# Scan groups of a hybrid decoder layer: rows spread over the partitions by transfers from memory in place of matmuls, with a new order inside a group

## The chip, the cores and the metric

The kernel runs on one core of a Trainium2 chip. The metric is the device time of one execution in microseconds (us), as the median of several runs. The engines are TensorE (PE; its weight loads are PEld), VectorE (DVE), ScalarE (ACT), GpSimd (POOL) and SyncE (SP), which issues nearly all DMAs from one queue, in program order. A wait in that queue holds back everything behind it. All data are float32, and each matmul of the program stands in the trace as two instructions.

## The reference, cut to what matters

One step of a decoder layer: 512 prompt tokens and 8 decode tokens (T = 520 columns) go through a sparse attention branch and a Mamba-2 scan branch, are merged, and pass a feed-forward block. The change is in the scan branch, which has 8 groups of 4 heads of 64 channels, with a state size of 128:

```python
xbc = silu(causal_conv(xbc_pad, conv_w, conv_b))          # x, B and C of the group, 4 taps
a_cum = cumsum(dt_c * A, axis=2)                          # in chunks of 128 tokens
L = exp(where(tri, a_cum[:, :, :, None] - a_cum[:, :, None, :], -inf))
CB = einsum('bclgn,bcsgn->bclsg', C_c, B_c)
y_diag = einsum('bclsg,bclsgr,bcsgrp->bclgrp', CB, L, xdt)
# chunk after chunk, h is the state:
y_off = einsum('blgn,bgrpn,blgr->blgrp', Ck, h, exp(ak))
h_new = h * exp(ak[:, -1]) + einsum('blgn,blgr,blgrp->bgrpn', Bk, exp(ak[:, -1:] - ak), xk)
# the 8 decode tokens, each with a state of its own:
h = h * exp(dtt * A) + einsum('bgrp,bgn,bgr->bgrpn', xt, Bt, dtt)
y = einsum('bgrpn,bgn->bgrp', h, Ct)
# both, per group:
y = (y + d_skip * xs) * silu(z)
y = y * rsqrt(mean(y * y over the group's 256 channels) + EPS) * ssm_norm_w
```

## The kernel before, in words

Everything lies transposed, channels on the 128 partitions and tokens in the columns. The order is written out by hand for each engine and held together by semaphores. The stages are: norm and first projections, index scores and top-k, attention, the 8 scan groups, the products with `w_ssm_br` (`sbr`) and the gates, decode attention, and then the output and feed-forward products.

**A group.** While the scan of group g is computed, PE also computes the six dense tiles of the input projection of group g+1 (x, x, B, C, z, z), 16 matmuls each, as filler between the steps of the scan: `D(i)` is tile i, `D(i, k0, k1)` a part of its eight k steps. Two pairs of PSUM banks alternate, so a tile starts only when ACT has copied out the tile before the last (`tile_in`; `gate_ahead` in the last group). In the last group the filler is tiles of the gate projection (`last_tile`). PE's steps are:

- `step_aux`: small transposes (raw columns, old convolution rows, the state `hT` of the group before), and, with the selector matrix `gs`, matmuls that put dt and decay of the decode tokens (L972, L973) and the decays at the chunk ends (L977) on all partitions.
- `step_norm` (L417) sums the squares of the group before. ACT takes the root, DVE the reciprocal, and `spread_norm` (L425, L426) puts the result on all partitions for DVE's `norm`.
- `step_turn` transposes B and x of the chunks (L994, L999).
- `step_decode` (L1011) puts each decode token's B row and C row on all partitions, in PSUM banks 6, 7 and 4, 5, where DVE reads them (L1849, L1860).
- `step_cb` (L1019) is CB of the four chunks, masked by DVE into `CBm`.
- `step_a` (L1028), once per chunk, puts four heads' cumulated decay rows on all partitions in bank 4. ACT's `chunk` makes from them `M2` (L1418, L1422) and `Cx2` (L1420); POOL multiplies these with `CBm` and C (L2243, L2246).
- `step_y` (L1041, L1044, L1047), once per chunk, makes the output and the state increment. DVE carries the state on (`hT`, L1878 and L1881), and the next `step_y` waits for that (`h_done`).

DVE does, in this order: copies of the group's constants, 12 convolution taps (L1811), the exponent of the chunk weights (L1815), four silu products (L1818), part of a round of the decode top-k (L1770, L1776, L1779; nobody in the group waits for its result), `norm` of the group before, `xdt` and `xw`, the rest of the round, the decode state update (L1849, L1854) and output (L1860, L1863), `CBm`, a second round, four carries of the state with `z_gate` ahead of the last, and the group's output `Y`. ACT's `squares`, POOL's `add_squares` and PE's `step_norm` follow on `Y`. POOL also does the decode tokens' convolution (L2222 to L2232) and the decay of the decode states (L2237).

SP stores the convolution rows and states, loads the next group's state, rows and selectors, and loads the weights of group g+2 when their slots are free.

Of the kernel before, what the change touches and what calls it, by code (L numbers as in the profile page):

```python
# [26 lines left out]
P = 128  # L27
D = 1024
# [48 lines left out]
def build(nc, x_prompt, x_sample, cache_k, cache_v, cache_idx_k, state_ssm, state_conv, page_table,  # L77
# [5 lines left out]
    with ExitStack() as ctx:  # L83
# [19 lines left out]
        gs = sb("gs", [32, GSEL])  # L103
        vec = sb("vec", [P, 96])
        cwg = sb("cwg", [P, NG, 24])
# [98 lines left out]
        scratch = nc.dram_tensor("decode_scores", (NB, PAST), F32, kind="Internal").ap()  # L204
        iqslot = [ikt3, ikt1]
# [34 lines left out]
        scl = scl[0:24, :]  # L240
        smallg, sa = W(sa, 512)
# [17 lines left out]
        cw = G(24)  # L259
        dtg, atg = G(4, 4), G(4, 4)  # L260
        sct = G(4, 24)
        sc0, sc1, sc2, sc3 = G(4, NB), G(4, NB), G(4, NB), G(4, NB)
        dts, dAs, xdts, ys = G(2, NB), G(2, NB), G(2, NB), G(2, NB)
        alast, ealast = G(4, 4), G(4, 4)
        wexp = G(4, 4)
# [96 lines left out]
        GIDX_READY, IK_READY, IDX_ZERO, WK_READY, MASK_READY, RAW_ZERO = 7, 8, 9, 10, 11, 12  # L362
        QK_NEW_READY, ROWS_READY, LK_READY, DMAX_READY, DP_READY, DO_READY = 13, 14, 15, 16, 17, 18

        VEC_READY, TAPS_READY, DSK_READY, IK_SQ, IK_ROOT, QKVS_READY, IKTOK_READY = 1, 2, 3, 4, 5, 7, 9
# [46 lines left out]
        def sum_squares(pe, e, *squares):  # L412

            for b in range(5):
                n = P if b < 4 else NB
                for i, sq in enumerate(squares):
                    mm = pe.matmul(ps[0:n, 6, b:b + 1], sq[:, b * P:b * P + n], ones[:, 0:1],  # L417
                                   start=(i == 0), stop=(i == len(squares) - 1))
            mm.then_inc(S("norm_summed"), 1)
# [9 lines left out]
        def root_norm(act, e, n):  # L429

            act.wait_ge(S("norm_summed"), e + 1)
            for rows, cols in ((P, slice(0, 4)), (NB, slice(4, 5))):
                act.activation(rt[0:rows, cols], ps[0:rows, 6, cols], ACT.Sqrt, scale=1.0 / n,
                               bias=eps[0:rows, 0:1]).then_inc(S("norm_root"), 1)
# [6 lines left out]
        def copy_norm(act, e, out):  # L441
            act.wait_ge(S("norm_spread"), e + 1)
# [92 lines left out]
        def _(sp):  # L535
            sp.sem_inc(S("sout_out"), OPEN)
            sp.dma_start(cst[:, 0:2 * P], consts[:, 0:2 * P]).then_inc(S("ident_in"), 16)
# [35 lines left out]

            sp.wait_ge(S("dsc_ready"), OPEN + 16)
# [56 lines left out]
            def load_selectors(g):  # L631
                sp.dma_start(gs[:], gsel_d[bass.ds(g, 1)].rearrange("o p c -> (o p) c")
                             if not isinstance(g, int) else gsel_d[g]).then_inc(S("gs_in"), 16)
# [3 lines left out]
            load_selectors(0)  # L637
# [6 lines left out]
            def group_io(g, more, last=False):  # L644

                store_conv(g)
# [12 lines left out]
                if not last:  # L659
                    sp.wait_ge(S("abc_done"), 4 * g + 4)  # L660
                    load_selectors(g + 1)

            group_io(0, True)
            with sp.Fori(1, NG - 2) as g:
                store_prompt_state(g - 1)
                group_io(g, True)
            store_prompt_state(NG - 3)
# [4 lines left out]
            store_prompt_state(NG - 2)  # L672
# [8 lines left out]
            load_sbr(0, (N_SBR + 2, N_SBR + 4))  # L681
            store_prompt_state(NG - 1)
# [32 lines left out]
            load_ga(3, N_SBR + 14)  # L715
            load_att(0, N_SBR + 16)
# [37 lines left out]
        def _(pe):  # L754
# [204 lines left out]
            def step_aux(g, prev):  # L959
# [3 lines left out]
                if prev:  # L963
                    pe.wait_ge(S("h_done"), 4 * g)
                for i in range(4):
                    mm = pe.transpose(ps[0:11, 5, i * P:(i + 1) * P], raw[:, i, SEQ:SEQ + 11], ident)
                mm.then_inc(S("ctok_done"), 1)
                pe.wait_ge(S("scl_in"), 48 * g + 48)
                pe.wait_ge(S("gs_in"), 16 * g + 16)
                for j in range(2):  # L970
                    sel = gs[:, 512 + j * P:512 + (j + 1) * P]
                    pe.matmul(ps[:, 4, 96 + NB * j:96 + NB * (j + 1)], sel, dtT[0:32, SEQ:T], start=True, stop=True)  # L972
                    pe.matmul(ps[:, 4, 112 + NB * j:112 + NB * (j + 1)], sel, acT[0:32, SEQ:T], start=True, stop=True)  # L973
                for i in range(4):
                    mm = pe.transpose(ps[:, 4, i * 24:(i + 1) * 24], scl[:, i * P:(i + 1) * P], ident[0:24, 0:24])
                for r in range(4):
                    mm = pe.matmul(ps[:, 4, 384 + 4 * r:388 + 4 * r], gs[:, r * P:(r + 1) * P], acT[0:32, P - 1:SEQ:P],  # L977
                                   start=True, stop=True)
# [5 lines left out]
            def step_norm(g):  # L984

                pe.wait_ge(S("sqg_added"), g + 1)
                sum_squares(pe, g + 1, sqg[:, 0, :])

            def step_turn(g, prev):
# [5 lines left out]
                if prev:  # L995
                    pe.wait_ge(S("norm_copied"), 2 * g + 2)
# [6 lines left out]
            def step_decode(g):  # L1003

                pe.wait_ge(S("xdt_ready"), 2 * g + 2)
                pe.wait_ge(S("Bt_ready"), g + 1)
                pe.wait_ge(S("aux_read"), g + 1)
                pe.wait_ge(S("silu_done"), 4 * g + 4)
                for t, bank in ((2, 6), (3, 4)):
                    for b in range(NB):  # L1010
                        mm = pe.matmul(ps[:, bank + b // 4, (b % 4) * P:(b % 4 + 1) * P],  # L1011
                                       xc[:, t, SEQ + b:SEQ + b + 1].broadcast_to((P, P)), ident,
                                       start=True, stop=True)
# [1313 lines left out]
```

## Time and profile before

| | |
|---|---|
| median of 3 runs | 1694.37 us (1694.1 to 1696.58) |
| the profiled execution, its own time | 1695.87 us |
| its span, first to last instruction | 1694.1 us |
| PE busy | 1602.1 us, 95% of the span |
| DVE busy | 1007.6 us, 59% |
| ACT, POOL busy | 369.8 us, 218.4 us |
| mean granted TensorE clock | 0.965 of full speed |
| DMA | 131.14 MB, 77 GB/s over the span |

The span and the median are nearly the same, so a microsecond in the trace is a microsecond of the metric. A timeline row gives start, duration, engine, line, operation and operands, and in brackets the idle time ahead of it with the engine that ended it. Rows of PE overlap the next by about 0.07 us, since the ends of matmuls are modelled, so the start-to-start distance is the better cost.

### The profile page before, as it was taken

To read this page: it belongs to the slowest core of one execution; us is meant where nothing else is said; L and a number is where in the kernel's file an instruction comes from. 1 tells how busy PE (TensorE), PEld (TensorE's weight loads), DVE (VectorE), ACT (ScalarE), POOL (GpSimd) and SP (SyncE) were. 2 spreads that over 40 slices of the span, in tenths; PEclk is the share of its full clock that TensorE was granted. 3 is DMA by queue.
4 is the path that set the end of the run, shared out by engine and by line. 5 is a ranking of instruction groups with operands and counts; after the bars stand their busy time and mean duration, and the time that the engine had idled before them with its cause. 6 is when DMAs were issued, how large, how long until landed. Compare 5 with 4: busy or idle time off the path is not lost. (4 is left out here: it accounts for less than half of the span.)

```text
span 1694.1 us, 21865 instructions
## 1 busy us (share of the span) xinstructions
PE 1602.1 (95%) x8083; PEld 1356.9 (80%) x8083; DVE 1007.6 (59%) x1640; ACT 369.8 (22%) x817; POOL 218.4 (13%) x224
## 2 busy tenths in 40 slices
PE   6998998899999999999989999999999999999997
PEld 5886786788877787777877788888888888888885
DVE  3313886336868667686775897403786666667222
ACT  3112316422343433424232100010011000000002
POOL 1000110021322413224132000520000000000000
PEclk7999999999999999999999999978999999999997
DMA  6111114033133121331122322421322323220301
GB/s 207 50 38 51 37 51 115 12 91 100 57 104 101 57 74 57 101 88 48 50 82 75 123 79 75 138 86 55 96 75 75 99 74 99 75 92 21 129 9 51
DMA packets 153486, 131.14 MB, mean 77 GB/s; under 512 B 11411, under 2 KB 149939, under 8 KB 153411
## 3 DMA queue, kind: packets, MB, share of 16 engines
q1 hardware_dynamic: 150610, 121.93, 23.7%
q0 software_dynamic: 2816, 8.39, 1.7%
q8 instruction: 41, 0.67, 0.2%
q14 instruction: 19, 0.15, 0.0%
HBM read 117.26 MB, written 13.27 MB: 77 GB/s over the span
## 5 line engine op out<-in xcount | busy, mean ns | idle before, releaser
L389 PE MATMUL ps<-xn,ring 128*128 128x260 f32 (+1 forms) x2752 | 638.1, 389 | 6.0 <-ACT work L1316 1.9
L389 PEld LDWEIGHTS ps<-xn,ring 128*128 128x128 f32 (+1 forms) x2752 | 522.9, 193 | 91.9 <-ACT work L1316 2.3
L469 PE MATMUL ps<-uT,ssm_o 128*128 128x260 f32 x616 | 139.5, 383 | 0.1
L469 PEld LDWEIGHTS ps<-uT,ssm_o 128*128 128x128 f32 x616 | 117.0, 190 | 18.4 <-issue 0.4
L389 PE MATMUL ps<-ssm_o,ring 128*128 128x260 f32 x512 | 114.0, 386 | 0.0
L389 PEld LDWEIGHTS ps<-ssm_o,ring 128*128 128x128 f32 x512 | 98.3, 192 | 15.3
L469 PE MATMUL ps<-xn,ring 128*128 128x260 f32 x392 | 94.0, 383 | 0.0
L2243 POOL TENSOR_TENSOR ring<-ring 128x512 f32<-128x512 f32 x32 | 40.5, 1266 | 334.0 <-ACT ring L1422 334.0
L469 PEld LDWEIGHTS ps<-xn,ring 128*128 128x128 f32 x392 | 74.3, 190 | 11.4
L506 ACT ACTIVATE work<-ps 128x260 f32<-128x260 f32 x34 | 13.0, 381 | 321.8 <-PE ps L469 239.8
L1878 DVE TENSOR_TENSOR work<-work 128x256 f32<-128x256 f32 x24 | 18.0, 749 | 93.5 <-PE ps L1047 93.5
L1770 DVE MAX8 work<-work 8x8 f32<-8x2049 f32 x32 | 72.9, 2278 | 0.9 <-issue 0.4
L1776 DVE FIND_INDEX8 dix<-work 8x8 uint32<-8x2049 f32 x32 | 72.8, 2274 | 0.0
L1779 DVE MATCH_REPLACE8 work<-work 8x2049 f32<-8x2049 f32 x32 | 72.5, 2267 | 0.0
L512 DVE TENSOR_TENSOR work<-work,ps 128x260 f32<-128x260 f32 x34 | 14.4, 425 | 97.7 <-PE ps L469 97.7
L1811 DVE SCALAR_TENSOR_TENSOR work<-work 128x512 f32<-128x512 f32 x96 | 67.0, 768 | 7.3 <-ACT work L1432 7.3
L469 PE MATMUL ps<-uT,ring 128*128 128x260 f32 x280 | 68.8, 390 | 0.4 <-DVE uT L1982 0.4
L469 PE MATMUL ps<-work,ring 128*128 128x260 f32 x280 | 64.6, 382 | 0.0
L469 PE MATMUL ps<-xn,ssm_o 128*128 128x260 f32 x264 | 62.2, 383 | 0.3 <-DVE ssm_o L2111 0.3
L469 PEld LDWEIGHTS ps<-uT,ring 128*128 128x128 f32 x280 | 54.2, 194 | 9.0 <-DVE uT L1982 0.5
L469 PEld LDWEIGHTS ps<-work,ring 128*128 128x128 f32 x280 | 53.2, 190 | 8.2
L469 PEld LDWEIGHTS ps<-xn,ssm_o 128*128 128x128 f32 x264 | 50.1, 190 | 8.4 <-issue 0.7
(356 smaller groups left out, 2207.9 us busy)
## 6 DMA issues: line engine op xcount, KB each, us to landing
ring<-in_w_in SPq DMA_DIRECT2D x34, 1024.0 KB, 5.3
ring<-in_w_ffn_gate SPq DMA_DIRECT2D x11, 1024.0 KB, 5.2
ring<-in_w_ffn_up SPq DMA_DIRECT2D x11, 1024.0 KB, 5.4
ring<-in_w_in SPq DMA_DIRECT2D x16, 512.0 KB, 5.3
work<-in_state_ssm SPq DMA_DIRECT2D x16, 512.0 KB, 6.5
out<-work SPq DMA_DIRECT2D x16, 512.0 KB, 4.0
ring<-in_w_ssm_br SPq DMA_DIRECT2D x8, 1024.0 KB, 7.9
ring<-in_w_ffn_down SPq DMA_DIRECT2D x8, 1024.0 KB, 5.2
```

The lines of the kernel that those rows point to most:

```text
L389: mm = pe.matmul(ps[0:m, 2 * pair + h, 0:TH], lhs[k], rhs[k][:, h * TH:(h + 1) * TH], start=(k == 0), stop=(k == len(lhs) - 1))
L469: mm = pe.matmul(ps[:, bank, 0:TH], ws[k], rs[k], start=(k == 0), stop=(k == len(ws) - 1))
L506: act.activation(d[:, 0, 0:TH], ps[:, 0, 0:TH], ACT.Copy).then_inc(S("p1_copied"), 1)
L512: v.tensor_tensor(d[:, 1, 0:TH], d[:, 0, 0:TH], ps[:, 1, 0:TH], ALU.add).then_inc(S("quarter_sums"), 1)
L1770: v.max(dm8[0:NB, :], smp[0:NB, :]).then_inc(S("dtop_max"), 1)
L1776: v.max_index(dix[:], dm8[0:NB, :], smp[0:NB, :]).then_inc(S("dtop_index"), 1)
L1779: v.match_replace(smp[0:NB, :], dm8[0:NB, :], smp[0:NB, :], -3.3e38).then_inc(S("dtop_cut"), 1)
L1811: v.scalar_tensor_tensor(xc[:, i, 0:SEQ], raw[:, i, t:t + SEQ], cw[:, 5 * i + t:5 * i + t + 1], xc[:, i, 0:SEQ], ALU.mult, ALU.add).then_i ...
L1878: v.tensor_tensor(hT.rearrange("p (r q) -> p r q", q=64), hT.rearrange("p (r q) -> p r q", q=64), ealast[:, :, c:c + 1].broadcast_to((P, 4 ...
L2243: g.tensor_tensor(m, m, CBm[:, c:c + 1, :].broadcast_to((P, 4, P)), ALU.mult).then_inc(S("M_ready"), 1)
```

## The change

Four things come to the partitions by DMA from scratch tensors in memory, where matmuls did it: the decay rows of a group (`load_decays`, 128 copies of 8 KB), the decode tokens' B and C rows (`spread_rows`: two transposes on PE, a copy by ACT, 8 KB out to memory, 128 copies of 8 KB back in), the root of the group norm (`root_out` with 520 runs of 4 bytes, `root_in` with 128 copies of 2 KB), and, once for all groups ahead of them, the chunk ends and the decode steps' dt and decay, which now lie with the constants in `cwg` (120 columns per group for 24). The selector matrix and its loads are gone. The copies of decay, B and C rows lie in the space of `xT`, which is therefore saved to memory and loaded again before the output products. The order of steps in a group is new on PE, DVE, ACT and SP: the decode update on DVE stands among the carries of the state, the top-k rounds after it, `tile_in` of tile 0 ahead of the tanh operations, `z_gate` at the group's start, and `step_norm` uses a corner of bank 4 and waits for ACT's copies out of that bank.

```diff
 SP, once, after the head:
+            sp.wait_ge(S("a_summed"), 4)
+            sp.dma_start(ac_d.rearrange("g (r t) -> (g r) t", t=SEQ), acT[0:32, 0:SEQ]).then_inc(S("rows_out"), 16)
...
+            sp.dma_start(xT_d, xT_flat).then_inc(S("xT_moved"), 16)
+            sp.wait_ge(S("rows_out"), 16 * 6)
+            sp.wait_ge(S("cwg_ready"), 12)
+            sp.dma_start(cwg[:, :, 56:72], al_d.partition_broadcast(P)).then_inc(S("rows_in"), 16)
...
+            def load_decays(g):
+                src = ac_d[g] if isinstance(g, int) else ac_d[bass.ds(g, 1)].rearrange("o c -> (o c)")
+                sp.dma_start(abc_flat, src.partition_broadcast(P)).then_inc(S("abc_in"), 16)
...
-            def load_selectors(g):
...
+            def spread_rows(g, prev):
+
+                if prev:
+                    sp.wait_ge(S("C_used"), 2 * g)
+                sp.wait_ge(S("bct_copied"), g + 1)
+                sp.dma_start(bc_d.rearrange("t b n -> b t n"), bct[0:NB]).then_inc(S("bct_out"), 16)
+                if prev:
+                    root_out(g)
+                sp.wait_ge(S("bct_out"), 16 * g + 16)
+                sp.dma_start(BC, bc_d.partition_broadcast(P)).then_inc(S("bcast_in"), 16)
+                if prev:
+                    root_in(g)
+
+            def root_out(n):
+
+                sp.wait_ge(S("norm_recip"), 2 * n + 2)
+                with nc.allow_non_contiguous_dma(reason="one root a token"):
+                    sp.dma_start(rn_d[0, 0:SEQ].rearrange("(b p) -> p b", p=P), rt[:, 0:4]).then_inc(S("root_out"), 16)
+                    sp.dma_start(rn_d[0, SEQ:T].rearrange("(p o) -> p o", o=1), rt[0:NB, 4:5]).then_inc(S("root_out"), 16)
+
+            def root_in(n):
+                sp.wait_ge(S("root_out"), 32 * n + OPEN)
+                sp.dma_start(rbg, rn_d[0].partition_broadcast(P)).then_inc(S("root_in"), 16)
 SP, group_io:
+                if prev:
+                    store_prompt_state(g - 1)
                 ws = group_weights(g + 2) if more else iter(())
                 next(ws, None)
+                spread_rows(g, prev)
                 store_state(g)
                 next(ws, None)
                 if not last:
                     sp.wait_ge(S("state_out"), 32 * g + 32)
                     sp.wait_ge(S("C_used"), 2 * g + 2)
                     load_state(g + 1)
+                    sp.wait_ge(S("abc_read"), 4 * g + 4)
+                    load_decays(g + 1)
 SP, later:
             load_sbr(0, (N_SBR + 2, N_SBR + 4))
+            root_out(NG)
+            root_in(NG)
...
+            sp.dma_start(xT_flat, xT_d).then_inc(S("xT_moved"), 16)
 PE:
-                    pe.matmul(ps[:, 4, 96 + NB * j:96 + NB * (j + 1)], sel, dtT[0:32, SEQ:T], start=True, stop=True)
...
+            def step_rows(g, prev):
+
+                if prev:
+                    pe.wait_ge(S("norm_root"), 2 * g + 2)
...
+                for t in range(2):
+                    mm = pe.transpose(ps[0:NB, 4, t * NS:(t + 1) * NS], xc[:, 2 + t, SEQ:T], ident)
+                mm.then_inc(S("bct_turned"), 1)
...
-            def step_a(g, c):
...
                 step_aux(g, prev)
                 D(0, 4, 8)
                 if prev:
+                    pe.wait_ge(S("sct_ready"), g + 1)
+                    pe.wait_ge(S("sout_ready"), g)
                     step_norm(g - 1)
                 D(1)
-                if prev:
-                    spread_norm(pe, g)
+                D(2, 0, 4)
                 step_turn(g, prev)
-                D(2)
-                step_decode(g)
+                step_rows(g, prev)
+                D(2, 4, 8)
+                step_cb(g)
                 D(3)
-                step_cb(g)
-                step_a(g, 0)
-                D(4, 0, 4)
-                step_a(g, 1)
-                D(4, 4, 8)
                 step_y(g, 0)
+                D(4, 0, 5)
+                step_y(g, 1)
+                D(4, 5, 8)
                 D(5, 0, 2)
-                step_a(g, 2)
-                D(5, 2, 4)
-                step_y(g, 1)
-                D(5, 4, 5)
-                step_a(g, 3)
-                if more:
-                    D(5, 5, 8)
                 step_y(g, 2)
+                D(5, 2, 7)
                 step_y(g, 3)
-                if not more:
-                    D(5, 5, 8)
+                D(5, 7, 8)
 ACT, group: tile_in(g + 1, 0), four tanh, tile_in(g + 1, 1), root_norm, Bt, then
+                act.activation(bct[0:NB], ps[0:NB, 4, 0:2 * NS].rearrange("p (t n) -> p t n", n=NS),
+                               ACT.Copy).then_inc(S("bct_copied"), 1)
+                chunk(g, 0)
                 if more:
                     tile_in(g + 1, 2)
...
+                chunk(g, 1)
                 if more:
                     tile_in(g + 1, 3)
...
+                chunk(g, 2)
                 if more:
                     tile_in(g + 1, 4)
...
                 chunk(g, 3)
 DVE, group, from CBm on:
+                v.wait_ge(S("bcast_in"), 16 * g + 16)
+                state(0)
+                state(1)
+                state_y(0)
+                carry(0)
+                state_y(1)
+                if prev:
+                    norm(g - 1)
+                carry(1)
+                top_index(GROUP_ROUNDS * g)
+                top_cut(GROUP_ROUNDS * g)
+                carry(2)
+                top_max(GROUP_ROUNDS * g + 1)
+                top_index(GROUP_ROUNDS * g + 1)
+                carry(3)
+                top_cut(GROUP_ROUNDS * g + 1)
```

## Rows read from the trace of the kernel before

**Rows 1.** The page, busy time of the engines.

```profile
PE 1602.1 (95%) x8083; PEld 1356.9 (80%) x8083; DVE 1007.6 (59%) x1640; ACT 369.8 (22%) x817; POOL 218.4 (13%) x224
```

**Rows 2.** Windows: group 3, a piece of it, the end of the groups.

```profile
core 0: us, PE busy (x) PEld busy (x) DVE busy (x) ACT busy (x) POOL busy (x), PEclk, DMA share, GB/s
640.89:712.26 71.37, 66.89 (x387) 56.37 (x386) 51.29 (x64) 25.09 (x57) 19.42 (x18) 0.98 0.28 78
663.71:666.33 2.62, 2.62 (x14) 2.51 (x13) 2.16 (x3) 0.67 (x2) 0.00 (x0) 0.50 0.02 7
929.41:940.35 10.94, 7.12 (x35) 6.06 (x34) 3.88 (x10) 3.79 (x7) 1.28 (x1) 0.81 0.00 0
```

**Rows 3.** Timeline of PE in that group.

```profile
644.93 0.38 PE L972 MATMUL ps<-work,gs 32*128 32x8 f32 x2
...
646.10 1.03 PE L977 MATMUL ps<-work,gs 32*128 32x4 f32 x8
...
662.22 1.16 PE L425 MATMUL ps<-cst,rt 128*128 128x128 f32 x8 [3.10 <-DVE rt L439]
...
663.71 1.12 PE L994 MATMUL ps<-cst,work 128*128 128x128 f32 x4
...
673.62 3.73 PE L1011 MATMUL ps<-cst,work 128*128 128x128 f32 x32
...
685.73 1.15 PE L1028 MATMUL ps<-work,gs 32*128 32x128 f32 x8
686.81 3.77 PE L389 MATMUL ps<-xn,ring 128*128 128x260 f32 x16
...
710.68 0.45 PE L1041 MATMUL ps<-ring,xdt 128*64 128x128 f32 x4 [1.10 <-DVE work L1881]
```

**Rows 4.** Timeline of DVE there.

```profile
641.56 0.42 DVE L1881 TENSOR_TENSOR work<-work,ps 128x256 f32<-128x256 f32 x1
...
646.24 8.42 DVE L1811 SCALAR_TENSOR_TENSOR work<-work 128x512 f32<-128x512 f32 x12 [0.88 <-ACT work L1432]
654.59 1.86 DVE L1815 TENSOR_TENSOR work<-work 128x16 f32<-128x16 f32 x1
...
662.16 2.28 DVE L1770 MAX8 work<-work 8x8 f32<-8x2049 f32 x1
...
675.67 1.23 DVE L1849 TENSOR_TENSOR ring<-ps,work 128x1024 f32<-128x1024 f32 x1 [1.81 <-PE ps L1011]
676.93 1.23 DVE L1854 TENSOR_TENSOR work<-work,ring 128x1024 f32<-128x1024 f32 x1
...
703.12 1.34 DVE L1878 TENSOR_TENSOR work<-work 128x256 f32<-128x256 f32 x1 [6.07 <-PE ps L1047]
```

**Rows 5.** Timeline of ACT there.

```profile
644.21 1.25 ACT L1427 ACTIVATE work<-work 128x520 f32<-128x520 f32 x2 [6.58 <-DVE work L1892]
...
649.03 0.36 ACT L1445 ACTIVATE ring<-ps 128x256 f32<-128x256 f32 x1
...
654.20 1.16 ACT L1453 ACTIVATE work<-work 128x520 f32<-128x520 f32 x2 [4.75 <-POOL work L2232]
```

**Rows 6.** Timeline of POOL there.

```profile
654.07 4.75 POOL L2237 TENSOR_TENSOR work<-work 128x1024 f32<-128x1024 f32 x2
690.57 1.26 POOL L2243 TENSOR_TENSOR ring<-ring 128x512 f32<-128x512 f32 x1 [31.76 <-ACT ring L1422]
```

**Rows 7.** DMA issues: count, size, median us from issue to landing.

```profile
ring<-in_w_in SPq DMA_DIRECT2D x34, 1024.0 KB, 5.3
...
work<-in_state_ssm SPq DMA_DIRECT2D x16, 512.0 KB, 6.5
...
out<-ring SPq DMA_DIRECT2D x8, 128.0 KB, 1.8
...
decode_scores<-work SPq DMA_DIRECT2D x1, 64.0 KB, 3.0
...
pgb<-in_page_table SPq DMA_DIRECT2D x1, 64.0 KB, 3.2
```

**Rows 8.** Timeline of DVE after the groups.

```profile
1054.90 0.70 DVE L1908 SCALAR_TENSOR_TENSOR work<-work 128x520 f32<-128x520 f32 x1 [8.43 <-ACT work L1512]
```

More of the change, by code:

```diff
@@ L572, in _ @@
             sp.dma_start(iqsw[64:P].rearrange("p j b -> p (j b)"), iqs[0:64].rearrange("p j b -> p (j b)")).then_inc(S("iqs_swapped"), 16)
+            sp.wait_ge(S("a_summed"), 4)
+            sp.dma_start(ac_d.rearrange("g (r t) -> (g r) t", t=SEQ), acT[0:32, 0:SEQ]).then_inc(S("rows_out"), 16)
+            with nc.allow_non_contiguous_dma(reason="the chunks' last decays and the decode steps, once"):
+                sp.dma_start(al_d.rearrange("g (r c) -> (g r) c", c=4), acT[0:32, P - 1:SEQ:P]).then_inc(S("rows_out"), 16)
+                for i, rows in enumerate((dtT, acT)):
+                    for h in range(2):
+                        sp.dma_start(pk_d[i, h].rearrange("g (j b) -> (g j) b", b=NB),
+                                     rows[h:32:2, SEQ:T]).then_inc(S("rows_out"), 16)
+            sp.wait_ge(S("xT_ready"), 9)
+            sp.wait_ge(S("norm_ready"), KT)
+            sp.dma_start(xT_d, xT_flat).then_inc(S("xT_moved"), 16)
+            sp.wait_ge(S("rows_out"), 16 * 6)
+            sp.wait_ge(S("cwg_ready"), 12)
+            sp.dma_start(cwg[:, :, 56:72], al_d.partition_broadcast(P)).then_inc(S("rows_in"), 16)
+            for i in range(2):
+                for h in range(2):
+                    sp.dma_start(cwg[64 * h:64 * h + 64, :, 88 + 16 * i:104 + 16 * i],
+                                 pk_d[i, h].partition_broadcast(64)).then_inc(S("rows_in"), 16)
+            sp.wait_ge(S("xT_moved"), 16)
+            def load_decays(g):
+                src = ac_d[g] if isinstance(g, int) else ac_d[bass.ds(g, 1)].rearrange("o c -> (o c)")
+                sp.dma_start(abc_flat, src.partition_broadcast(P)).then_inc(S("abc_in"), 16)
+            load_decays(0)
             sp.wait_ge(S("dsc_ready"), OPEN + 16)
@@ L1364, in _ @@
                 act.activation(kvtok[0:n, b, :], ps[0:n, bank, :], ACT.Copy).then_inc(S("kvtok_copied"), 1)
+            act.wait_ge(S("vector_mark"), TABLE_READY)
+            for o in (56, 72, 104):
+                act.activation(cwg[:, :, o:o + 16], cwg[:, :, o:o + 16], ACT.Exp).then_inc(S("head_read"), 1)
             with act.Fori(0, NH // 2) as k:
@@ L1479, in group @@
                     gate_ahead(4)
-                chunk(g, 2)
                 chunk(g, 3)
@@ L1679, in _ @@
             v.wait_ge(S("tok_copied"), 3)
+            v.wait_ge(S("actok_ready"), 1)
+            for o, rows in ((24, tok[:, 0:4, 0:32]), (40, actok)):
+                chain(v.tensor_copy(cwg[:, :, o:o + 16].rearrange("p g (c r) -> p g c r", r=4),
+                                    rows.rearrange("p c (g r) -> p g c r", r=4)))
             v.wait_ge(S("vector_mark"), IDX_ZERO)
```

215 lines of the change are left out of this document (91 added, 124 removed).

## The prediction

> **What bounds the kernel now.** I read the page's busy times first: PE is busy for 95% of the span, DVE for 59% [rows 1]. Then the windows of one group in steady state: group 3 takes 71.4 us, of which PE is busy for 66.9, DVE for 51.3, ACT for 25.1 and POOL for 19.4, and the DMA engines are busy for 0.28 of it [rows 2]. So a group is bound by PE. The timeline of PE shows two waits in it of a microsecond or more: 3.10 us until DVE has the reciprocal of the norm, and 1.10 us until DVE has carried the state [rows 3]. After the first of them the granted clock is 0.50, the lower of the two levels (1.2 GHz for 2.4), for the 2.6 us of the turn [rows 2, 3]. That costs some 1.3 us per group. PE's own work at full speed is therefore about 65.6 us.
>
> **What the change takes from PE.** By start-to-start distances in rows 3, per group: the decay rows cost 1.08 us for each of four chunks, 4.3; the B and C rows 3.6; the selector matmuls of the auxiliary step, four at 0.23 and four at 0.24, 1.9; the spread of the norm 1.5 (662.22 to 663.71). That is 11.3 us. The 3.10 us wait ahead of the spread goes as well. Added are two transposes of B and C of the decode tokens, 0.5 us at the 0.27 of such a pair of instructions. PE alone would then need 71.4 - 11.3 - 4.4 + 0.5 = 56.2 us, or 54.9 with no half-speed piece.
>
> **What comes onto other engines.** DVE loses the exponent of the chunk weights and two copies (1.86 us and 0.3 [rows 4]) and keeps the rest, some 49 us of work. So DVE is now as close to the bound as PE, and what decides is the loop through both. I walk it with zero at the end of the fourth state carry of the group before.
>
> *To the norm sums.* Before, ACT's last copy out of bank 4 ended at 649.39, 7.4 us after that carry (641.98) [rows 4, 5]. In the new order a cut of the top-k (2.4 us, as the 2.28 of MAX8 [rows 4]) stands between the carry and the group's output, so `sout_ready` comes at 9.8. PE, which has only the first tile and two small steps to do, is there at about 6 and now waits for this copy ahead of `step_norm`: the wait removed at the spread comes back here, some 3 to 4 us long. I therefore keep the 1.3 us of half clock. Behind this wait stand PE's tile 1 and the turn, and DVE, SP and ACT all wait for the turn.
>
> *To the transfer.* Norm sums 1.0, tile 1 7.4, half clock 1.3, half of tile 2 3.7 (3.77 for 16 instructions [rows 3]), turn 1.3 at full clock, two transposes 0.5: 25.0. The tanh and silu steps do not delay this: tile 0's copy, now first, waits for POOL's convolution, as the tanh did before (4.75 us [rows 5]), and they end near 21.5, with POOL's decay (4.75 us [rows 6]) still in their way. ACT copies the eight rows: 25.4. SP stores them, waits for the reciprocal, issues the two root transfers (they stand ahead of B and C in the queue) and waits for the store: 1.8 us is what a store of 128 KB took, 3.0 one in 2048 runs of 32 bytes [rows 7]. The load of B and C is issued at about 28.5. Nothing in this trace reads 8 KB 128 times. A load of 1 MB in runs of 1 KB took 5.3 us, one of 512 KB in runs of 512 bytes 6.5 [rows 7]. I take 5.3, since size and runs are nearest, and 0.7 for what is queued ahead: B and C are there at 34.5. DVE has nothing to do from about 27.5 but `CBm`.
>
> *To the next carry.* Eight operations of 1024 elements at 1.26 start to start [rows 4] are 10.1 us, the first carry 0.45, three more at 0.9, `norm` 1.4, and the two stretches of top-k between carries 4.7 each. Together 24.0. B and C are now read from SBUF. L1815, 16 elements, took 1.86 us while POOL's decay ran, and L1878 took 1.34 us under POOL's products (0.42 without them), while L1854 took 1.23 with POOL idle [rows 4, 6]: an operation with two SBUF inputs waits out POOL's. The multiplications by B and C had one input in PSUM and become of that kind. POOL's pair for chunk 2 falls among them: 1.2 us, taken as one of its operations (1.26 [rows 6]). Sum 25.2, so the next mark is at 59.7. The Trainium skill, SBUF — State Buffer, section "Who interferes with whom", says the same: a VectorE instruction with two SBUF inputs is blocked for the whole of a GpSimd instruction that reads SBUF. Without that rule the loop would be 58.5 us; the trace agrees with the rule.
>
> PE's waits at the later steps are small in this walk (the second `step_y` 0.5 us), and `chunk` on ACT runs ahead, as its input is in SBUF since the group before. The load of the next decays is issued after chunk 3, over 30 us before its use; weights and states keep their slots. So a group costs 59.7 for 71.4: 11.7 us less, in all eight 93.6.
>
> **Outside the groups.** At the end 10.9 us lie between the last `step_y` and the first product with `w_ssm_br` [rows 2]. The spread there, about 2.5 us with its wait, goes. The root now takes two transfers (3.0 and 3.2 [rows 7], with issue and DVE's product 8.7), of which fourteen of the first tile's sixteen k steps cover 6.4 and the transposes 0.5; PE waits about 1.1. Net 1.4 less. DVE starts the remaining top-k rounds 5 us later with respect to PE; it waited 8.43 us for a tile near their end [rows 8], which covers that. If it did not, up to 5 us come on top. In the head DVE gets two copies and a subtraction and ACT three small exponents, in a stage where DVE sets the pace: 1.0 more. Saving and reloading `xT` (2 MB each way) cost nothing, in stages whose queue waits for PE and tens of microseconds ahead of the use; uncovered they would cost about 10 us each. Sum: 93.6 + 1.4 - 1.0 = 94.0. The profiled execution took 1695.9, so 1601.9, and the median of the runs lies 1.5 below it: **1600 us**.
>
> **Bounds.** The store 1.8 or 3.0, the load 5.3 or 6.5: -1 to +2.4 us per group. The blocking 0 to 3.7 (three of POOL's operations): -1.2 to +2.5. Half clock 0 or twice: -1.3 to +1.3. Not all at once: 57.7 to 62.5 per group, 1584 to 1622.
>
> **Rivals.**
> - *PE stays the bound.* If the copies out of bank 4 come early enough and the transfer hides under `CBm`, a group costs PE's 56.2 us: 8 x 15.2 less, 1574. For it: DVE's waits sum to 20 us in a group of now. Against: the cut and the transfer stand in series in the loop.
> - *The load of B and C is slow.* All 128 copies come from the same 8 KB. At some 10 us for it a group costs 64.5 and the kernel 1639. The Trainium skill, DMA: Bandwidth & Descriptors, section "Latency and other measured facts", reports copies whose partitions step in unison through memory at half rate, and suspects that they meet in one memory channel. By its 103 GB/s the load would take about 10 us, the same case. Nothing here shows it for this pattern.
> - *It is very slow, and the kernel slower than before.* The only load of this trace that copies one row to all partitions is the page table: 64 KB in 3.2 us, 1.4 above the shortest store [rows 7]. Were those 1.4 us all its data, sixteen times as much would take 22 us, landing in 24 for 5.3: 78.4 us per group, 56 slower in all, 1750. It decides from a landing time of 17 us on. Against it: other transfers of that size take 3 us too, so that most of it is not data.
> - *No change*: a landing time near 17 us by chance.
>
> **How the numbers follow.** The walk as it stands 0.60 (1584 to 1622), PE as bound 0.12 (near 1574), the half-rate load 0.17 (1622 to 1690), a load that costs more than is won 0.08, no change 0.03. A difference of over 0.2% (3.4 us) is about what a measurement of this kernel tells from none. Faster 0.89, same 0.03, slower 0.08. The range that leaves out no more than 0.2: 1572 to 1645.
>
> **What would show it.** Right: groups of about 60 us; PE idle 3 to 4 us ahead of the norm sums, released by ACT's L1445 copy; a half-clock piece behind it; DVE idle 6 us in two parts ahead of its first use of B and C, released by a DMA; L1849's successor at 1.26 us except beside POOL. Wrong: a landing time of B and C over 8 us; a wait of PE ahead of its third or fourth `step_y` for the carries; SP issuing the load of B and C late because it is held at the store or the root; or a wait for a reload of `xT`.

## The result, and the profile after

The changed kernel takes 1667.62 us (median of 4 runs, 1666.72 to 1669.19); beside it the kernel before took 1695.22. The ratio is 0.9842, with a 95% interval of 0.9827 to 0.9857: faster by 1.6%, where 5.6% was predicted (1600 us). 1667.6 lies above the range of 1572 to 1645. The profiled execution spans 1665.3 us, against 1694.1 before.

The page of the changed kernel, the lines that answer to [rows 1] and [rows 7]:

```profile
PE 1525.6 (92%) x7379; PEld 1289.0 (77%) x7379; DVE 1012.1 (61%) x1619; ACT 360.8 (22%) x769; POOL 227.7 (14%) x224
...
L1083 PE MATMUL ps<-ring,xdt 128*64 128x128 f32 x256 | 30.1, 322 | 58.2 <-DVE work L1908 58.2
...
L1889 DVE TENSOR_TENSOR ring<-xT,work 128x1024 f32<-128x1024 f32 x16 | 25.3, 1579 | 83.1 <-DMA xT<-decode_rows 82.9
...
xT<-decay_rows SPq DMA_DIRECT2D x8, 1024.0 KB, 4.7
...
xT<-decode_rows SPq DMA_DIRECT2D x8, 1024.0 KB, 13.0
```

PE's work fell by 76.5 us, but PE gained a wait that was not there: 58.2 us in front of the second `step_y` (L1083), for DVE's first carry. DVE in turn stood still for 82.9 us until the load of B and C had landed. The last two lines are the finding in short. Both loads spread 1 MB from a few rows in memory to all partitions; one lands in 4.7 us, the other in 13.0.

What is different about the second shows in SyncE's queue. Its timeline in a steady group (start, duration, what is issued):

```profile
641.91 0.31 SPq L673 DMA_DIRECT2D decode_rows<-ring  x1
643.77 0.37 SPq L685 DMA_DIRECT2D group_roots<-rt  x1
644.19 0.40 SPq L686 DMA_DIRECT2D group_roots<-rt  x1
644.73 0.34 SPq L677 DMA_DIRECT2D xT<-decode_rows  x1
654.95 0.33 SPq L690 DMA_DIRECT2D work<-group_roots  x1
```

L690, which reads the roots back, waits only for the two root writes. It is issued at 654.95, so these two small writes (2 KB in 512 words, and 8 words) took over 10 us. The load of B and C, issued half a microsecond behind them, lands only after they are done. The same stretch in windows (us, busy times of the engines, granted clock, share of the DMA engines, GB/s), with the piece after PE's wait, the first group and the last:

```profile
644.73:654.95 10.22, 10.22 (x57) 8.61 (x56) 0.69 (x1) 5.15 (x14) 3.76 (x3) 1.00 0.26 35
656.00:658.00 2.00, 2.00 (x10) 1.54 (x9) 0.13 (x1) 0.15 (x1) 1.77 (x2) 1.00 0.80 320
666.47:672.50 6.03, 6.03 (x26) 4.89 (x27) 5.96 (x8) 0.00 (x0) 0.00 (x0) 0.51 1.07 277
364.74:416.56 51.82, 51.82 (x287) 43.74 (x286) 43.71 (x48) 17.90 (x41) 20.21 (x17) 1.00 0.48 144
824.33:904.07 79.74, 58.77 (x296) 48.24 (x294) 53.31 (x67) 26.30 (x54) 21.04 (x19) 0.85 0.24 66
619.35:687.45 68.10, 57.91 (x299) 48.11 (x298) 51.76 (x62) 24.46 (x51) 20.26 (x18) 0.90 0.41 115
```

For 10 us 35 GB/s move, then 320: the load was held back, it was not slow for the whole of its time. Group 0 has no roots to write; its load landed in 4.7 us, and from its auxiliary step to that of the next group it took 51.82 us. The steady group takes 68.10 (71.37 before, [rows 2]). DVE and PE in it:

```profile
657.87 1.92 DVE L1889 TENSOR_TENSOR ring<-xT,work 128x1024 f32<-128x1024 f32 x1 [11.58 <-DMA xT<-decode_rows]
659.83 1.22 DVE L1893 TENSOR_TENSOR work<-work,ring 128x1024 f32<-128x1024 f32 x1
...
684.17 0.42 DVE L1913 TENSOR_TENSOR work<-work,ps 128x256 f32<-128x256 f32 x1
```

```profile
666.47 0.70 PE L1083 MATMUL ps<-ring,xdt 128*64 128x128 f32 x4 [8.29 <-DVE work L1908]
...
669.44 6.00 PE L400 MATMUL ps<-xn,ring 128*128 128x260 f32 x20
...
694.19 1.02 PE L428 MATMUL ps<-cst,work 128*128 128x1 f32 x8 [1.91 <-ACT ring L1481]
```

DVE waits 11.58 us. PE has two tiles to go on with and then waits 8.29. It loses more behind that wait: the granted clock is 0.51, the lower level, for the next 6 us (third row), and twenty instructions of the projection take 6.00 us that take 4.55 elsewhere.

At the end of the groups the last roots make the same way with nothing in front of them:

```profile
899.77 1.99 PE L428 MATMUL ps<-cst,work 128*128 128x1 f32 x10 [7.28 <-POOL work L2260]
...
904.07 17.12 PE L400 MATMUL ps<-ssm_o,ring 128*128 128x260 f32 x67
904.22 0.41 SPq L686 DMA_DIRECT2D group_roots<-rt  x1
913.46 0.33 SPq L690 DMA_DIRECT2D work<-group_roots  x1
...
917.69 1.43 DVE L1844 SCALAR_TENSOR_TENSOR ssm_o<-work,cwg 128x520 f32<-128x520 f32 x2 [13.91 <-DMA work<-group_roots]
```

Of DVE's 13.91 us, 9.24 are the writes (904.22 to 913.46) and 4.2 the read back. The DMA packets of this stretch, in 40 slices of 0.275 us from 903 to 914 (busy share in tenths, then their number), show where those 9.24 us do not go:

```profile
DMA  0000005300000000000000000000000000000000
...
DMA packets 544, 0.00 MB, mean 0 GB/s; under 512 B 544, under 2 KB 544, under 8 KB 544
```

By these records all 544 packets of the two writes run between 904.65 and 905.20. The semaphore that L690 waits for is full only at 913.46, some 8 us later. So the time lies between the packets as recorded and the report that the writes are complete. In the steady group the same view (644 to 658, slices of 0.35 us, GB/s) shows the load behind them start late and trickle, before it runs at 335 to 421 GB/s:

```profile
GB/s 0 0 6 0 0 0 0 0 0 0 0 94 70 23 47 47 47 47 23 23 0 47 0 47 23 0 47 23 140 211 47 23 351 421 421 404 335 372 250 143
```

### The profile page after: what moved, and what is told of

Same layout as the page of the kernel before. It is cut to its first block and busy times, and to the rows that moved or that the text cites. A ratio compares the mean times of both kernels' runs of the same rounds, so it can differ in the third digit from the quotient of the medians.

```text
span 1665.3 us, 20374 instructions
## 1 busy us (share of the span) xinstructions
PE 1525.6 (92%) x7379; PEld 1289.0 (77%) x7379; DVE 1012.1 (61%) x1619; ACT 360.8 (22%) x769; POOL 227.7 (14%) x224
## 5 line engine op out<-in xcount | busy, mean ns | idle before, releaser
L400 PE MATMUL ps<-xn,ring 128*128 128x260 f32 (+1 forms) x2752 | 648.9, 396 | 8.0 <-ACT work L1445 2.0
L400 PEld LDWEIGHTS ps<-xn,ring 128*128 128x128 f32 (+1 forms) x2752 | 537.4, 197 | 99.1 <-issue 4.4
L1083 PE MATMUL ps<-ring,xdt 128*64 128x128 f32 x256 | 30.1, 322 | 58.2 <-DVE work L1908 58.2
L1889 DVE TENSOR_TENSOR ring<-xT,work 128x1024 f32<-128x1024 f32 x16 | 25.3, 1579 | 83.1 <-DMA xT<-decode_rows 82.9
L1860 DVE SCALAR_TENSOR_TENSOR work<-work 128x512 f32<-128x512 f32 x96 | 75.7, 860 | 0.0
L1083 PEld LDWEIGHTS ps<-ring,xdt 128*64 128x64 f32 x256 | 17.6, 152 | 69.5 <-DVE work L1908 52.3
```

The costliest lines, as they stand in the source:

```text
L400: mm = pe.matmul(ps[0:m, 2 * pair + h, 0:TH], lhs[k], rhs[k][:, h * TH:(h + 1) * TH], start=(k == 0), stop=(k == len(lhs) - 1))
L1083: pe.matmul(o, xdt[:, c, 64 * r:64 * r + 64], M2[:, c % 2, r * P:(r + 1) * P], start=True, stop=(c == 0))
L1860: v.scalar_tensor_tensor(xc[:, i, 0:SEQ], raw[:, i, t:t + SEQ], cw[:, 5 * i + t:5 * i + t + 1], xc[:, i, 0:SEQ], ALU.mult, ALU.add).then_i ...
L1889: v.tensor_tensor(t2, BC[:, 0], xdts[:, j, :].unsqueeze(2).broadcast_to((P, NB, NS)), ALU.mult).then_inc(S("B_used"), 1)
```

## Experiments

Two theories first. *Q*: the writes of single words hold the load of B and C behind them. *L*: a spread load of rows written a moment before is slow by itself. A group's length is the distance between the auxiliary steps of two groups (L1028 of the changed kernel); "writes" is the time between the issue of the second root write and that of the read back in the tail, behind the last group, where no other transfer is issued in between. e3, e4, e5, e6, e10 and e12 ran once each; the four executions of e1 spread over 6 us and those of e9 over 9 us.

**e1, the load first.**

```diff
-                if prev:
-                    root_out(g)
                 sp.wait_ge(S("bct_out"), 16 * g + 16)
                 sp.dma_start(BC, bc_d.partition_broadcast(P)).then_inc(S("bcast_in"), 16)
                 if prev:
+                    root_out(g)
                     root_in(g)
```

> The load that spreads the decode rows of B and C to all partitions is issued before the two transfers that write the group's roots to memory. Nothing is left out. Theory Q (the 520 four-byte writes of the roots stand ahead of the load in SyncE's queue and hold it): the load lands in 4.7 to 5.5 us in all eight groups instead of 13.0, VectorE's wait for it falls from 11.6 us to about 3.5, a group goes from 68.1 to 59.5 to 61 us, and the time is 1668 less 7 x 7.5 to 8.3, so 1608 to 1615 us. Theory L (a spread load of rows that were written a moment before is slow by itself): the landing stays 12 to 14 us and the time within 0.3% of the changed kernel, 1662 to 1673 us.

1603.59 us (1601.67 to 1607.94), ratio to before 0.9466 [0.945, 0.9483]. The load lands in 4.7 us at the median (4.3 to 4.8 in seven groups, 8.0 in the last). Its queue, DVE's wait and a group:

```profile
674.12 0.35 SPq L675 DMA_DIRECT2D xT<-decode_rows  x1
674.65 0.36 SPq L685 DMA_DIRECT2D group_roots<-rt  x1
675.05 0.40 SPq L686 DMA_DIRECT2D group_roots<-rt  x1
685.17 0.33 SPq L690 DMA_DIRECT2D work<-group_roots  x1
```

```profile
678.99 1.23 DVE L1889 TENSOR_TENSOR ring<-xT,work 128x1024 f32<-128x1024 f32 x1 [1.81 <-DMA xT<-decode_rows]
```

```profile
647.18:707.16 59.98, 56.60 (x300) 47.24 (x299) 53.49 (x62) 24.57 (x51) 22.20 (x18) 0.94 0.43 130
```

The writes still take 10.1 us, but nobody waits for them within the group. Two lines of order are worth 64 us. Theory L is out. The time lies 4 us below Q's interval: groups 1 to 4 take 56.3 to 58.3 us, where 59.5 to 61 was expected, and only groups 5 and 6 reach 60.0 and 60.2.

**e2, the roots by TensorE.** The five products that spread the norm go behind those of C and B, into bank 5, and ScalarE copies them:

```diff
                 step_cb(g)
+                if prev:
+                    pe.wait_ge(S("Bt_ready"), g + 1)
+                    pe.wait_ge(S("xdt_ready"), 2 * g + 2)
+                    spread_norm(pe, g, at=(5, 0))
                 D(3)
...
-                v.wait_ge(S("root_in"), 16 * g + 16)
+                v.wait_ge(S("norm_copied"), 2 * g + 4)
```

> The group roots reach all partitions by TensorE and a copy of ScalarE again (five one-row products right after the products of C and B, copied by ScalarE in its idle time), so no root goes through memory; decay rows and the decode rows of B and C still do, and the new order stays. Nothing is left out. Theory Q: landing 4.7 to 5.5 us, a group of 59 to 61 us, and the tail without its 13.9 us wait for the last root's rows, about 8 to 10 us shorter: 1600 to 1608 us. Theory L: landing stays 12 to 14 us, and only the tail gains: 1655 to 1662 us.

1595.86 us (1594.57 to 1596.42), ratio 0.941 [0.9394, 0.9425]; landing 4.6 us; groups with roots of 58.3 to 60.5. The tail gains as well: DVE's wait there is 3.39 us for ScalarE's copy, not 13.91. The time is 4 us below the interval expected by Q.

**e3, e7: the roots in 128 runs of 16 bytes.** e3 changes only the pattern; e7 puts the right token into each run by summing every fourth one.

```diff
-sp.dma_start(rn_d[0, 0:SEQ].rearrange("(b p) -> p b", p=P), rt[:, 0:4])
+sp.dma_start(rn_d[0, 0:SEQ].rearrange("(p b) -> p b", b=4), rt[:, 0:4])
```

> As the changed kernel, but the roots of the prompt are written in 128 runs of 16 bytes, one a partition, in place of 512 runs of 4 bytes: the roots then stand at other tokens' places, so the group norms use wrong tokens' roots; all else is computed as before. If the cost of these writes goes by their number (136 in place of 520), they take 3 to 4 us in place of about 10, the load of B and C lands in 6 to 7 us, a group is 61 to 62 us and the time 1617 to 1625 us. If it goes by something that does not shrink with the number (the queue's fixed costs, waiting for the load before), landing stays at 12 to 13 us and the time near 1665 us.

e3: 1599.47 us, landing 6.0, writes 1.21. The direction was as expected, the size was not: writes of 3 to 4 us and a time of 1617 to 1625 were expected.

> The roots in 128 runs of 16 bytes with nothing left out: the sums of squares take every fourth token, so that partition q holds the roots of tokens 4q to 4q + 3, and its four words go to memory in one piece at their right places. Order as in the changed kernel. If a strided stationary operand costs TensorE nothing that shows, the time is that of the run with wrong places, 1596 to 1603 us; else up to 4 x 0.3 us a group more, 1606 to 1612 us. Theory L would still say about 1665 us.

e7: 1607.86 us (1605.92 to 1608.15), ratio 0.9485 [0.9465, 0.9505], landing 6.1. The strided operand has a price. The norm sums' lines of e3's sister with words apart (e4, contiguous operand) and of e7:

```profile
L429 PEld LDWEIGHTS ps<-cst,work x90: 85/192/337, 423.5 to 1165.5; 128*128 128x128 f32 x72, 128*8 128x8 f32 x18
```

```profile
L429 PEld LDWEIGHTS ps<-cst,work x90: 85/329/330, 423.6 to 1179.0; 128*128 128x128 f32 x72, 128*8 128x8 f32 x18
```

A weight load takes 329 ns at the median for 192. In all, the 72 full-size loads of this line are busy 16.5 us in e7 and 10.0 us in e3, 6.5 more. From the first group's auxiliary step to the last group's e7 takes 414.4 us for e3's 407.6, 6.8 more. So the loads account for most of the 8 us between the two times, though that each added microsecond lies on the path is argued, not shown.

**e4, e5, e6, e10: words apart, and fewer words.** In all four the decode roots get a row of their own and the read back takes another row, so that only the 512 (or 128) root words differ.

```diff
-rn_d = nc.dram_tensor("group_roots", (1, T), F32, kind="Internal").ap()
+rn_d = nc.dram_tensor("group_roots", (1, K * SEQ), F32, kind="Internal").ap()
...
+sp.dma_start(rn_d[0].rearrange("(b p s) -> p b s", p=P, s=K)[:, :, 0:1], rt[:, 0:4].unsqueeze(2))
```

with K = 16 (64 bytes) in e4, 4 in e5, 1 in e6; e10 is e6 with `rt[:, 0:1]` alone.

> As the changed kernel, but each of the 512 four-byte writes of the roots goes 64 bytes from its neighbour in memory, and the load that should bring the roots back reads a row of decay sums instead: the group norms use wrong factors, all else is computed as before. The number of writes is the same. If what costs is that many small writes fall into the same few lines of memory, the writes take 3 to 4 us, the load of B and C lands in 6 to 7 us and the time is 1617 to 1625 us. If it is the number of small writes, the landing stays at 12 to 14 us and the time within 0.4% of 1668 us.

> As the run in which the root words went 64 bytes apart (writes done within some 1.5 us of their issue, landing of the B and C load 5.5 us, 1595 us), but 16 bytes apart, so that four of the 512 words share 64 bytes; the group norms again use wrong factors, all else is computed. If the cost goes by how many words written one by one share the same 64 bytes (16 in the changed kernel, about 10 us; 1 in that run, about 1.5 us), this stands between: writes 2 to 4 us, landing 5.5 to 8 us, time 1595 to 1618 us. If any sharing costs the whole, landing is 12 to 14 us and the time near 1660 us.

> The control for the runs with words apart: the 512 root words adjacent as in the changed kernel, but, as in those runs, the eight decode roots go to a row of their own and the load that should bring the roots back reads a row of decay sums (the group norms use wrong factors, all else is computed). If adjacency is what costs, the landing of the B and C load is 12 to 14 us and the time 1655 to 1670 us. If it was the decode roots' transfer into the same row, or the read back, the landing is 5 to 6 us and the time near 1595 us.

> As the run with adjacent words and the read back redirected, but only 128 of the 512 root words are written (the first column; the group norms use wrong factors in both): still 16 words in each 64 bytes, but in 8 such pieces of memory in place of 32. If the cost is the queueing of the 16 writes that share one piece, with the pieces side by side in time, the landing of the B and C load stays at 12 to 14 us and the time near 1670. If it goes by the number of adjacent words, the landing is 6 to 8 us and the time 1597 to 1615 us.

| run | small writes a group | words in 64 bytes | writes us | landing us | time us |
|---|---|---|---|---|---|
| changed kernel | 520 | 16 | 9.24 | 13.0 | 1667.62 |
| e6 | 520 | 16 | 9.67 | 13.6 | 1670.37 |
| e10 | 136 | 16 | 7.21 | 12.5 | 1662.08 |
| e5 | 520 | 4 | 2.26 | 6.4 | 1607.54 |
| e4 | 520 | 1 | 1.47 | 5.5 | 1594.99 |
| e3 | 136 (128 of 16 bytes) | 16, in 4 writes | 1.21 | 6.0 | 1599.47 |

The tail of e4 and of e10, from which the column of the writes comes (e3, e5 and e6 are read alike):

```profile
842.01 0.41 SPq L687 DMA_DIRECT2D group_roots_decode<-rt  x1
843.48 0.35 SPq L691 DMA_DIRECT2D work<-decay_rows  x1
```

```profile
900.75 0.33 SPq L687 DMA_DIRECT2D group_roots_decode<-rt  x1
907.96 0.34 SPq L691 DMA_DIRECT2D work<-decay_rows  x1
```

The number of writes alone does not set the cost: 520 of them take 1.5 us when apart, 136 take 7.2 us when adjacent, and the fourfold number adjacent takes 9.7. What sets it is how densely words, each written by itself, lie in memory: 16, 4 and 1 in 64 bytes give 7.2 to 9.7, 2.3 and 1.5 us. The four 16-byte writes of e3 in 64 bytes cost no more than e5's four words, rather less.

That 64 bytes is the piece that counts is not shown. Counted in pieces of 512 bytes the writes are 128, 32 and 8 for the three spacings, 128 for e10 and 32 for e3, which orders the runs just as well.

Of the expectations, e5, e6 and e10 came out about as expected (e6's time 0.4 us above its interval, e10's 8 us below its 1670). e4 and e3 were expected at 1617 to 1625 us and came out 22 and 18 us below 1617, since a group with the load on time is shorter than the expectations had it.

The Trainium skill, DMA: Bandwidth & Descriptors, section "Specifications", says that a write below 512 bytes is done as a read and a write back. The runs do not contradict it, but by size alone all six rows would be alike; they differ eightfold.

That writes into the same piece of memory wait for one another is the likeliest reading, and argued. The packets themselves take no longer. Here is e4's view of its tail, 841 to 844 in slices of 0.075 us:

```profile
DMA  0000000000000000000058783000000000000000
```

Its packets, 544 as well, run from 842.50 to some 842.95, and L691 is issued at 843.48, half a microsecond later, where the changed kernel needs 8 us more after as short a burst. Which part of the path behind the packets makes the adjacent writes wait no run here shows.

**e9, e12: another queue.** The root writes go into ScalarE's queue. In e9 the load of B and C is issued 0.5 us before them, in e12 0.5 us after (SyncE waits for one count of `bct_out` more, which ScalarE gives behind them: the last line of the diff, of e12 alone).

```diff
                                ACT.Copy).then_inc(S("bct_copied"), 1)
+                if prev:
+                    act.wait_ge(S("norm_recip"), 2 * g + 2)
...
+                    act.dma_start(rn_d[0, 0:SEQ].rearrange("(b p) -> p b", p=P), rt[:, 0:4]).then_inc(S("root_out"), 16)
+                    act.dma_start(rn_d[0, SEQ:T].rearrange("(p o) -> p o", o=1), rt[0:NB, 4:5]).then_inc(S("root_out"), 16)
+                act.sem_inc(S("bct_out"), 16)
```

> The two transfers that write the group's roots are issued from ScalarE's queue, right after its copy of B's and C's decode rows, at about the time at which SyncE issues the load of B and C; all else as in the changed kernel and nothing left out. If the writes hold only what stands behind them in their own queue, the load lands in 4.7 to 6 us, a group takes 58 to 61 us and the time is 1600 to 1612 us. If they hold the DMA engines themselves (or the memory), the load of the other queue waits too: landing 9 to 14 us and the time 1640 to 1670 us.

> As the run with the root writes in ScalarE's queue, but SyncE's load of B and C now waits until ScalarE has issued them, so that the writes stand ahead of it in time, as in the changed kernel, though in another queue (there the load was issued 0.5 us before the writes, so it told only that a load that goes first is free). Nothing is left out. If the writes hold only their own queue, the load lands in 4.7 to 6 us and the time is 1605 to 1617 us (the load itself goes some 1 us later than in that run). If they hold the DMA engines or the memory for every queue, the load lands in 10 to 14 us and the time is 1645 to 1670 us.

e9: 1611.71 us (1606.85 to 1615.6), ratio 0.9502 [0.9477, 0.9526], landing 4.7; that it is 8 us above e1 was not followed up. e12: 1662.54 us, landing 13.2 (its groups with roots 66.9 to 68.7 us). Of e12, ScalarE's queue and SyncE's:

```profile
645.34 0.37 ACTq L1507 DMA_DIRECT2D group_roots<-rt  x1
645.74 0.43 ACTq L1508 DMA_DIRECT2D group_roots<-rt  x1
```

```profile
646.25 0.35 SPq L675 DMA_DIRECT2D xT<-decode_rows  x1
655.47 0.33 SPq L688 DMA_DIRECT2D work<-group_roots  x1
```

So theory Q was too narrow. The writes hold not their queue but what both queues share, the DMA engines or the memory, and only what is issued behind them in time. By the packets above the writes do not keep the engines busy; the load behind them trickles at 23 to 94 GB/s. What blocks it there stays open. e9 by itself would have misled: it is fast only because its load goes first.

**e8, e11: VectorE's steps moved into its wait.** The index and cut steps of the first selection round go before the wait for B and C, the second cut behind the next group's first copy; e8 on e2, e11 on e7 with the load first.

```diff
+                top_index(GROUP_ROUNDS * g)
+                top_cut(GROUP_ROUNDS * g)
                 v.wait_ge(S("xdts_ready"), g + 1)
                 v.wait_ge(S("bcast_in"), 16 * g + 16)
...
                 carry(1)
-                top_index(GROUP_ROUNDS * g)
-                top_cut(GROUP_ROUNDS * g)
-                carry(2)
                 top_max(GROUP_ROUNDS * g + 1)
+                carry(2)
                 top_index(GROUP_ROUNDS * g + 1)
                 carry(3)
-                top_cut(GROUP_ROUNDS * g + 1)
```

> The version with the roots by TensorE, and VectorE's first index and cut step of a group's selection rounds done before it waits for the B and C load, where it was idle; the second cut moves to the start of the next group. Nothing is left out. If, after the wait is gone, VectorE's chain of work sets the group (60 us, of which about 1.6 to 2.7 us a group are the wait for the load and 1 to 2 us the moved steps), a group gets 2 to 4 us shorter: 1566 to 1580 us. If TensorE is the bound by then, the time stays within 0.3% of 1596 us.

> The best version that keeps every spread through memory: the B and C load first, the roots in 16-byte runs at their right places, and VectorE's index and cut steps before its wait for the load. Nothing is left out. Landing 4.7 to 5.5 us and a group, bound by TensorE as in the matmul version with the early steps (58.25 us), but without its five products (1.4 us) and with the slower strided sums (about 1 us): 57 to 59 us; time 1590 to 1602 us.

e8: 1596.5 us (1596.08 to 1597.77), ratio 0.9423 [0.9404, 0.9443]: nothing gained over e2. e11: 1600.53 us (1599.6 to 1603.05), ratio 0.9439 [0.9423, 0.9454]: the time as expected, with groups of 58.5 to 60.2 where 57 to 59 was expected. PE in a group of e8, its waits:

```profile
665.36 3.77 PE L400 MATMUL ps<-xn,ring 128*128 128x260 f32 x16 [0.92 <-ACT work L1418]
669.97 0.66 PE L1029 MATMUL ps<-cst,work 128*128 128x128 f32 x4 [0.84 <-DVE work L1858]
...
672.37 0.38 PE L1044 MATMUL ps<-cst,work 128*8 128x128 f32 x2 [0.87 <-ACT rt L444]
...
691.57 0.45 PE L1065 MATMUL ps<-ring,xdt 128*64 128x128 f32 x4 [0.41 <-DVE work L1901]
```

```profile
651.49:709.74 58.25, 55.22 (x310) 46.01 (x309) 50.60 (x62) 25.16 (x54) 25.84 (x18) 1.00 0.43 129
```

The wait ahead of the norm sums is gone and with it the half clock (1.00), but four waits of under a microsecond, 3.0 us in all, take its place: 55.2 of 58.25 us are PE's work. In a group of e2 PE is busy for 56.4 of 58.29 us and waits 1.91 once. So with the load on time PE's work is 95% of a group again; why the rest comes to the same length in both is not shown. e2 and e8 are the fastest versions that leave nothing out, and not told apart (0.6 us); e2 lies 71.8 us or 4.3% below the changed kernel.

## Why the prediction was wrong, and where it was right

The step that failed stands in *To the transfer*: "I take 5.3 [...] and 0.7 for what is queued ahead". The 5.3 was about right (4.7 of e1 and of group 0), and so was the moment of issue: 28.5 on the walk, 644.73 - 616.49 = 28.2 in the trace, with zero at the end of a fourth carry (684.59 less a group of 68.10). The 0.7 was about 8.3, so that B and C were there at 41.4 in place of 34.5. The same price was wrong a second time at the end of the groups, where the root writes took 9.24 us for 3.0. I had priced a store of small runs by one of 2048 runs of 32 bytes (3.0 us, [rows 7]) and took the 512 words for the same kind; the runs show that for single words the number counts little and the neighbours much.

What it costs: windows from the auxiliary step of group 0 to that of the last group, and from there to the first product with `w_ssm_br`, of the kernel before, of the changed kernel (its second one stands above) and of e1:

```profile
367.62:858.80 491.18, 464.35 (x2681) 389.92 (x2680) 355.21 (x441) 169.72 (x390) 134.12 (x125) 0.98 0.28 80
858.80:940.35 81.55, 70.69 (x393) 59.17 (x392) 50.42 (x65) 26.98 (x61) 20.75 (x19) 0.91 0.14 43
```

```profile
364.74:824.33 459.59, 397.02 (x2075) 330.31 (x2074) 355.17 (x416) 164.68 (x347) 141.81 (x125) 0.91 0.42 118
```

```profile
366.34:767.40 401.06, 383.32 (x2075) 320.72 (x2074) 363.45 (x414) 164.81 (x347) 155.39 (x125) 0.97 0.45 136
767.40:839.05 71.65, 54.38 (x296) 45.25 (x295) 54.98 (x70) 26.30 (x54) 22.00 (x19) 0.91 0.24 73
```

459.59 + 79.74 = 539.33 us in the changed kernel, 472.71 in e1: 66.6 us in the profiled executions, 64.0 between the medians, of the 67.6 by which the prediction was low.

*The rest of the walk, read from e1.* The group shown takes 59.98 for the predicted 59.7, with PE's work at 56.60 for 56.2 and 3.38 us ahead of the norm sums, released by ScalarE's copy L1481 as said. (The changed kernel itself shows 1.91 there.) But e1 has no steady group: its groups 1 to 6 take 56.3 to 60.2 us, 58.2 on average, and its group 2 runs at full clock with 53.7 us of PE's work. From DVE's first product with B to the fourth carry e1 takes 26.8 us, predicted 25.2. The two windows of e1 are 100.0 us shorter than those of before (572.73), where 95.0 were predicted (93.6 + 1.4). The stage from `w_ssm_br` on is 6.6 us longer (760.4 for 753.8), where nothing was charged, and the head 1.3 shorter, where 1.0 more was. So that e1 comes within 4 us of the predicted 1600 is in part luck: a group priced too high and an end priced too low make up for each other.

*The blocking by POOL.* In the changed kernel L1889 takes 1.92 us beside POOL's products and 1.22 without, which agrees with the Trainium skill, SBUF — State Buffer, "Who interferes with whom". With a state product (L1910) at 1.46 for 0.40 that is 1.8 us in the group shown, 1.2 predicted. In e1, where the load is on time, POOL's products for two chunks fall among DVE's:

```profile
680.25 2.17 DVE L1893 TENSOR_TENSOR work<-work,ring 128x1024 f32<-128x1024 f32 x1
682.45 2.18 DVE L1889 TENSOR_TENSOR ring<-xT,work 128x1024 f32<-128x1024 f32 x1
```

```profile
679.11 2.23 POOL L2292 TENSOR_TENSOR ring<-ring 128x512 f32<-128x512 f32 x1 [0.50 <-ACT ring L1461]
```

With a third at 2.03 us that is 2.7 us for the predicted 1.2, which covers the 1.6 us by which 26.8 exceeds 25.2. POOL's product takes 2.23 us for 1.27 too: each engine holds up the other.

*What bounds the group.* Argued as DVE's chain with PE close by. e8 says otherwise: DVE's cuts taken off the chain give nothing. The length of a group came out near all the same, because both chains were within 4 us.

*Outside the groups.* The head cost was put at 1.0; the groups began 2.9 us earlier (364.74 for 367.62). From the last `step_y` to `w_ssm_br` 12.6 us (891.45 to 904.07) for 10.9, not 1.4 less: PE waits 7.28 us there, 3.07 before, since the moved cut stands ahead of the group's output. Behind it the cover failed: with DVE 13.91 us behind instead of 8.7, PE waits 5.29 us at a later step for DVE's selection, 1.67 before, and the stage from `w_ssm_br` on takes 761.2 us for 753.8. The text had this as "up to 5 us come on top". (e1 waits 4.52 us there.)

*The rivals.* PE as the bound was put at 1574, which leaves out the terms outside the groups; with them it is 1572. The half-rate load gave 1639 with a landing at 10 us; the symptom (landing over 8 us) came, its cause did not: the load moves 1 MB in 4.7 us, over 220 GB/s, and the load of distinct rows took 5.3, so the pattern of the same 8 KB read 128 times costs nothing here, and the Trainium skill's rule on partitions in step (DMA: Bandwidth & Descriptors, "Latency and other measured facts") does not reach this one. The very slow load and its turning point of 17 us were not met. The list lacked the rival that came: a cheap-looking transfer ahead that is slow.

## What to carry to other kernels

Never write adjacent single words to memory one by one ahead of a transfer that something waits for: give each partition a run of 16 bytes, spread the words 64 bytes apart, or let TensorE spread them; another queue does not help. What the critical chain waits for is issued first, however small the rest is. And price a small transfer from a row with the same size of run and the same neighbours, or bound it by the issue of what waits for it.

## What the runs showed of the hardware

- 512 four-byte writes (with 8 more behind them) took 9.2 to 9.7 us when adjacent, 2.3 when 16 bytes apart, 1.5 when 64 bytes apart; 128 adjacent ones 7.2; the same 2 KB in 128 runs of 16 bytes 1.2. The DMA packets run in about half a microsecond whether adjacent or 64 bytes apart; after them it takes 8.3 us when adjacent, 0.5 when apart, until the transfer issued on their completion starts.
- During such adjacent writes a load of 1 MB issued behind them in either of two queues lands in 12.5 to 13.6 us; issued 0.5 us ahead of them it lands in 4.7.
- 8 KB in memory read by all 128 partitions (1 MB) lands in 4.6 to 4.7 us at the median where it goes first (the decay rows' load took 4.6 to 6.4 over the runs).
- A VectorE product of two SBUF operands (128x1024) took 2.03 to 2.18 us beside GpSimd's products and 1.22 alone, and GpSimd's product 2.23 for 1.27.
- A stationary operand (128x128) with a stride of four words loads in 329 ns at the median, against 192 without a stride.
